# Two score matmuls of a differential attention unit issued next to each other, into two PSUM banks

## The reference

```python
q = rms_norm(q.reshape(B_, S_, H, 2, dq), q_g) * dq ** -0.5      # H = 16 heads, 2 components, dq = 64
k = rms_norm(k.reshape(B_, S_, H, 2, dq), k_g)
def block(start):                                                # blocks of 128 queries
    ...
    s = jnp.einsum('ibhqd,ibhkd->ibhqk', qb, k).astype(f32) + bias
    s = jnp.where(allowed, s, -jnp.inf)                          # chunk-causal, chunks of 64
    pr = jax.nn.softmax(s, axis=-1)
    attn = pr[0] - lam * pr[1]
    return jnp.einsum('bhqk,bhkd->bhqd', attn, v)
```

## Time and profile before

| | |
|---|---|
| median of 3 runs | 2461.01 us (2460.45 to 2461.78) |
| the profiled execution | 2460.94 us |
| its span, first to last instruction | 2459.1 us |
| TensorE busy | 2438.4 us (99%) |
| VectorE busy | 1264.5 us (51%) |
| ScalarE busy | 1092.0 us (44%) |
| stage of groups 0 to 2 | 218.8 to 480.5 us |
| score passes (L598), all | 128, from 218.9 to 532.3 us |

### The profile page before, as it was taken

One profiled execution on the slowest core, in us unless ns is written; L12 is line 12 of the kernel. 1 busy time (PEld: TensorE's weight loads), 2 busy tenths in 40 slices (PEclk: granted clock), 3 DMA queues, 4 the chain that ended last, 5 costly groups with the idle time before them and its releaser, 6 DMA issues.

```text
span 2459.1 us, 28865 instructions
## 1 busy us (share of the span) xinstructions
PE 2438.4 (99%) x10818; PEld 1954.3 (79%) x10818; DVE 1264.5 (51%) x1513; ACT 1092.0 (44%) x1407; POOL 48.6 (2%) x60
## 2 busy tenths in 40 slices
PE   8999999999999999999999999999999999999999
PEld 6887777778888888888888888888888888888887
DVE  6555566655545444444444545655445444454443
ACT  6644545544444444443444454444444444433332
POOL 1000000000000000000000000000000000000000
PEclk9999999999999999999999999999999999999999
DMA  7564445445666666665656755556666666665664
GB/s 252 181 195 146 146 145 146 146 143 175 183 185 187 180 186 182 185 182 186 186 183 187 231 162 172 166 176 186 183 185 182 184 184 184 183 187 184 196 195 144
DMA packets 229577, 440.81 MB, mean 179 GB/s; under 512 B 14573, under 2 KB 16754, under 8 KB 229234
## 3 DMA queue, kind: packets, MB, share of 16 engines
q1 hardware_dynamic: 223186, 430.01, 58.3%
q10 hardware_dynamic: 6304, 9.61, 1.1%
HBM read 437.45 MB, written 2.12 MB: 179 GB/s over the span
## 4 chain that ended last, share of the span: by engine, by line
PE 97%; DVE 1%; ACT 1%; issue 0%; ACTq 0%; DMA 0%; POOL 0%; DVEq 0%
PE bank L454 31%; PE bank L452 30%; PE bank L453 30%; PE bank L472 2%; PE bank L598 1%; PE bank L625 1%; ACT w_hi L750 0%; PE bank L518 0%; PE bank L571 0%; DVE aT_lo L1159 0%; ACT aT_hi L787 0%; PE bank L611 0%; ACTq L1035 0%; DVE w_lo L1091 0%; DVE y L1131 0%
## 5 line engine op out<-in xcount | busy, mean ns | idle before, releaser
L1091 DVE TENSOR_TENSOR w_lo<-raw,w_hi 128x1024 fp32r<-128x1024 f32 x816 | 997.4, 1225 | 1131.1 <-ACT w_hi L750 1130.4
L750 ACT ACTIVATE w_hi<-raw 128x1024 fp32r<-128x1024 f32 x816 | 862.9, 1059 | 1243.8 <-PE bank L454 1238.3
L452 PE MATMUL bank<-w_hi,hT_hi 128*128 128x512 f32 x2112 | 840.9, 398 | 0.0
L454 PE MATMUL bank<-w_hi,hT_lo 128*128 128x512 f32 x2112 | 840.2, 398 | 0.0
L453 PE MATMUL bank<-w_lo,hT_hi 128*128 128x512 f32 x2112 | 832.9, 394 | 0.0
L452 PEld LDWEIGHTS bank<-w_hi,hT_hi 128*128 128x128 f32 x2112 | 396.7, 188 | 96.4 <-issue 4.0
L453 PEld LDWEIGHTS bank<-w_lo,hT_hi 128*128 128x128 f32 x2112 | 396.9, 188 | 96.2
L454 PEld LDWEIGHTS bank<-w_hi,hT_lo 128*128 128x128 f32 x2112 | 396.5, 188 | 92.5
L454 PE MATMUL bank<-w_hi,aT_lo 128*128 128x512 f32 x1152 | 458.5, 398 | 0.0
L452 PE MATMUL bank<-w_hi,aT_hi 128*128 128x512 f32 x1152 | 456.9, 397 | 0.8 <-DVE aT_lo L1159 0.8
L453 PE MATMUL bank<-w_lo,aT_hi 128*128 128x512 f32 x1152 | 454.9, 395 | 0.0
(11 more groups left out here) (96 smaller groups left out, 638.2 us busy)
## 6 DMA issues: line engine op xcount, KB each, us to landing
raw<-in_ffn_w_gate_dram SPq DMA_DIRECT2D x176, 512.0 KB, 3.7
raw<-in_ffn_w_up_dram SPq DMA_DIRECT2D x176, 512.0 KB, 3.6
raw<-in_ffn_w_down_dram SPq DMA_DIRECT2D x176, 512.0 KB, 4.3
raw<-in_a_w_in_dram SPq DMA_DIRECT2D x104, 512.0 KB, 3.7
raw<-in_b_w_in_dram SPq DMA_DIRECT2D x72, 512.0 KB, 3.8
raw<-in_a_w_out_dram SPq DMA_DIRECT2D x40, 512.0 KB, 3.8
raw<-in_b_w_out_dram SPq DMA_DIRECT2D x40, 512.0 KB, 4.3
raw<-in_mem_w_kv_dram SPq DMA_DIRECT2D x32, 512.0 KB, 4.6
```

The lines of the kernel that those rows point to most:

```text
L452: nc.tensor.matmul(o, hi[:, k, rows], w_hi[:, slot, a, :], start=(first and a == 0), stop=False)
L454: last = nc.tensor.matmul(o, lo[:, k, rows], w_hi[:, slot, a, :], start=False, stop=(last_one and a == CHUNK_KT - 1))
L750: nc.scalar.activation(w_hi[:, slot], raw[:, slot], ACT.Copy).then_inc(hi_ready, 1)
L1091: nc.vector.tensor_tensor(w_lo[:, slot], raw[:, slot], w_hi[:, slot].bitcast(F32), ALU.subtract).then_inc(chunk_split, 1)
```

## The change

In groups 0 to 2 (units 0 to 23, n < TAIL_FIRST) component 0 is written to bank 6 and component 1 to bank 7. Both matmuls are issued one behind the other at the end of the step's attention work, without `s_half` between them. They wait for `T_free`, `s_free` and now `at_copied`. VectorE reads component 1 from bank 7. Group 3 keeps its order, its one bank and `s_half`.

```diff
+TAIL_FIRST = (QT - 1) * GROUP_UNITS
...
+        def score_place(n, i):
+
+            if n >= TAIL_FIRST:
+                return bank[S_BANK][:, i * SEQ:(i + 1) * SEQ]
+            return bank[(S_BANK, AT_BANK)[i]][:, i * SEQ:(i + 1) * SEQ]
...
-            def diff_scores(n, i):
+            def diff_score(n, i):
                 h, t = DIFF_UNITS[n]
                 group = h // HPB
+                part = slice(i * QK, (i + 1) * QK)
+                return nc.tensor.matmul(score_place(n, i)[:, 0:(t + 1) * P],
+                                        qT[part, group % 2, h % HPB, t * P:(t + 1) * P],
+                                        kT[part, group % 2, h % HPB, 0:(t + 1) * P], start=True, stop=True)
+
+            def diff_scores(n):
+                wait(pe, T_free, tally.at("t"))
+                wait(pe, s_free, n)
+                pe.wait_ge(at_copied, FIRST_UNIT["diff"] + n)
+                diff_score(n, 0)
+                diff_score(n, 1).then_inc(s_done, 1)
+                asked["diff_scores"] = n + 1
+
+            def tail_scores(n, i):
                 if i == 0:
                     wait(pe, T_free, tally.at("t"))
                     wait(pe, s_free, n)
+                    diff_score(n, 0).then_inc(s_half, 1)
                 else:
-                    pe.wait_ge(s_half, n + 1)
...
+                    pe.wait_ge(s_half, n + 1 - TAIL_FIRST)
+                    diff_score(n, 1).then_inc(s_done, 1)
                 asked["diff_scores"] = n + 1
...
                 s, tr, o = steps_of(at)
                 first = group * GROUP_UNITS
-                if s is not None:
-                    diff_scores(first + s, 0)
+                tail = group == QT - 1
+                if tail and s is not None:
+                    tail_scores(first + s, 0)
...
                 if o is not None:
                     diff_output(first + o)
                 if s is not None:
-                    diff_scores(first + s, 1)
+                    if tail:
+                        tail_scores(first + s, 1)
+                    else:
+                        diff_scores(first + s)
...
-                            out=e_buf[:, u % 2, i, 0:keys], in0=bank[S_BANK][:, i * SEQ:i * SEQ + keys],
+                            out=e_buf[:, u % 2, i, 0:keys], in0=score_place(n, i)[:, 0:keys],
```

## The result

The median is 2444.8 us (2444.4 to 2445.8, 4 runs) against 2461.1 before: ratio 0.9934, 95% interval 0.9923 to 0.9946. The sign was right, the size was not.

What follows compares the result with a forecast made beforehand. TensorE, busy 99% of the span, was taken as the bound. Savings of 21 x 0.40 + 0.33 - 2 x 0.21 = 8.3 us plus 2.5 for overlap gave 10.8, so 2450.2 us; range 2448.3 to 2457.9.

Steps and rivals of the forecast that it cites:

- The sign: Whole kernel: the change makes it faster, chance 0.81; same 0.14, slower 0.05.
- The bound and the stage: Groups 0 to 2: TensorE bounds, busy 259.7 of 261.7 us; its savings count if no other engine becomes late.
- The switch price, 0.20 us, and two of four gone: TensorE, 23 of 24 units: each change between 64-row and 128-row form costs 0.20 us; two go, saving 0.40 per unit.
- the sum in strict turns: Score pairs: components strictly one after the other, second's weights loaded under the first; 8.3 us saved, 2452.7 us, chance 0.26.
- The s_half wait, 0 with an output between and 0.33 in unit 0: Between score components: dropping the wait saves nothing where an output lies between, 0.33 us once in unit 0.
- case E: Score pairs: the pair still costs unit 0's wait; 0.4 us saved, 2460.6 us, chance 0.05.
- Units 9 and 17: Outputs already waiting for y from VectorE: 0.21 us lost in each in place of 0.40 won.
- The earlier output and its at_T copy: Output moves 0.51 or 0.72 us earlier; its copy still lands in time, 0.27 us left at the tightest three.
- The overlap of the pair: Score pairs: second component starts with the first's second pass; 2.5 us more over 12 even units, nothing with 128 columns.
- the upper bound (12.1): Score pairs: weight loads overlap too, 1.3 us more; 12.1 us saved, 2448.9 us, chance 0.08.

Runs made afterwards that it cites:

- the kernel with no switches at all: Kernel before, but in groups 0 to 2 both score matmuls contract over all 128 partitions, components not kept apart: 2444.4 us, ratio 0.9932.

## Why the prediction missed

**The bound and the stage**: right. TensorE paid, nobody else became late, nothing was given back.

**The switch price, 0.20 us, and two of four gone**: right. The kernel with both components on one row half has the new order without overlap, and its stage is 8.15 shorter where the sum in strict turns said 8.3. The stage of the kernel with no switches at all is 16.2 shorter, for an expected 16.9.

**The s_half wait, 0 with an output between and 0.33 in unit 0**: right. Taken away alone it gave 0.82, 0.75 of it expected from unit 0; kept, it left 0.45 of the gain, for 0.4 in case E.

**Units 9 and 17**: right in kind. Their wait grew from 0.42 to 1.07 us. They came out even, not 0.21 worse, because the second component was free there too: with both on one row half unit 9's step is 2.66 us (311.25 to 313.91), 0.22 worse than the 2.44 before.

**The earlier output and its at_T copy**: right, no wait for it.

**The overlap of the pair**: this is the step that failed. The prediction took the second component to start with the first's second pass, "with one weight load of 0.11 at a time", worth 2.5 us in the units with 256 keys and nothing with 128. Even the upper bound (12.1) kept the passes in the order of issue and overlapped the loads only. Measured by the kernel on one row half against the kernel after, the overlap is worth 7.58 us: a whole component in each unit, 12 x 0.43 + 12 x 0.21 = 7.7. With 128 keys, too, the second component was free (0.49 us for four passes, as for two before). As read above, the first passes of both components start within 0.01 us, though the second pass of component 0 stands between them in the program. 8.15 + 7.58 is the 15.73 of the stage. So one term of the sum was mis-sized, 2.5 for 7.6, and its upper bound was no bound: it rested on an order that no row of before showed.

The Trainium skill's rule ("TensorE: Matmul & The Clock Gate", Part 3: Packing small matmuls) has matmuls on different row groups start some 4 ns apart; the rows here agree, with 0.01 us or less. The prediction bent it to its own order of passes. By the rule taken plainly, a pair costs what one component does, and the estimate is 8.3 + 7.7 = 16.0, against 15.73 measured in the stage.

What stays open: whether the pair would run side by side into one bank too. No run has the new order into one bank without the wait, so what the second bank is worth by itself is not shown.

## What to carry to other kernels

Read starts, not busy shares: TensorE stood at 99% before, and 16 us of that were switches between the 64-row and the 128-row form and a component that could have run beside another. Matmuls with 64 rows belong next to each other on different halves, without a wait between them (here also into different banks). The new order with the wait kept gave 0.45 us of the stage, the second bank without the wait in the old order 0.82, and together they gave 15.73. And when bounding an overlap from above, take it as complete unless a row forbids it.

## What the runs showed of the hardware that was not expected

Two fp32 matmuls of two passes each, on different row halves, run pass beside pass: 0.70 us for all four passes with 256 columns, as for one matmul alone, weight loads included (two in 0.19, where one takes 0.18). On the same half the same four passes take 1.13 us. The passes, as inferred from their starts, don't keep the order in which the matmuls were issued: both first passes start within 0.01 us, 0.31 or more ahead of any second one. A change of form costs 0.20 us, and not changing it was worth as much (16.2 us of the stage) as the whole of the change studied.
